# The order of the last loads, finished rows and block halves at the end of a diffusion block with mixture of experts

## The reference

```
x  = x + gx1 * mixer(rmsnorm(x) ...)                 # pooling mixer and gated linear attention
hx = rmsnorm(x, norm2) * (1 + cx2) + sx2
s  = sigmoid(hx @ w_router)                          # 16 experts, top 2 of one group
xb = rows of hx sorted by expert, padded to blocks of 128
yb = (silu(xb @ w1[e]) * (xb @ w3[e])) @ w2[e]       # for each block, e its expert
x  = x + gx2 * (for each token the weighted sum of its two rows of yb)
out = rmsnorm(x, norm_f)
```

## Time and profile before

| | |
|---|---|
| median of 3 runs | 892.17 us (891.77 to 892.59) |
| profiled execution | 892.63 us, its span 890.9 us |
| busy: TensorE, VectorE | 858.4 us (96%), 635.9 us (71%) |
| busy: ScalarE, GpSimd | 415.1 us (47%), 194.5 us (22%) |
| chain that ended last, by engine | PE 78%, DVE 11%, DMA 5% |
| mean granted clock | 0.984 |

### The profile page before, as it was taken

How to read it: one execution, slowest core, us unless ns; L and a number is a source line. 1 busy time by engine, 2 the same in 40 slices (tenths; PEclk the granted TensorE clock), 3 DMA queues, 4 the chain that set the end, 5 groups by cost and what they waited for, 6 DMA issues and landing times.

```text
span 890.9 us, 14102 instructions
## 1 busy us (share of the span) xinstructions
PE 858.4 (96%) x4980; PEld 706.8 (79%) x4981; DVE 635.9 (71%) x907; ACT 415.1 (47%) x597; POOL 194.5 (22%) x225
## 2 busy tenths in 40 slices
PE   8999999999999999999879999999999999999993
PEld 6789878888997567887678888888888888888872
DVE  1678755789777748556875769399936648599995
ACT  3485456201224441232253457378634525487772
POOL 4042001100000101111033323233313222234324
PEclk9999999999999999999969999999999999999997
DMA  9953566511035032222799759979997596699984
GB/s 342 344 179 110 171 194 211 152 43 57 8 142 191 1 142 81 109 79 102 261 338 329 245 170 370 303 245 379 377 361 255 174 307 220 176 342 379 370 331 177
DMA packets 82359, 195.31 MB, mean 219 GB/s; under 512 B 4919, under 2 KB 13324, under 8 KB 82314
## 3 DMA queue, kind: packets, MB, share of 16 engines
q1 hardware_dynamic: 71168, 158.87, 49.6%
q0 software_dynamic: 8272, 25.84, 11.2%
q10 hardware_dynamic: 2874, 10.01, 2.8%
HBM read 169.57 MB, written 25.71 MB: 219 GB/s over the span
## 4 chain that ended last, share of the span: by engine, by line
PE 78%; DVE 11%; DMA 5%; issue 2%; ACT 2%; POOL 1%; ACTq 0%; SPq 0%; POOLq 0%; DVEq 0%
PE ps L2455 16%; PE ps L2443 12%; PE ps L2104 9%; PE ps L2460 8%; PE ps L2107 7%; PE ps L2437 2%; PE ps L2304 2%; DMA raw<-in_w_dram 2%; PE ps L2295 1%; DVE arena L1420 1%; PE ps L2297 1%; PE ps L2296 1%; DMA raw<-x_rows 1%; PE ps L2246 1%; PE ps L2160 1%
## 5 line engine op out<-in xcount | busy, mean ns | idle before, releaser
L1144 ACT ACTIVATE wah<-raw 128x2048 fp32r (+1 forms) x32 | 61.4, 1919 | 65.6 <-issue 32.8
L1853 DVE TENSOR_TENSOR wbl<-raw,wbh 128x2048 fp32r<-128x2048 f32 x32 | 73.1, 2288 | 5.2 <-ACT wbh L1144 4.5
L2443 PE MATMUL ps<-w2h,hTh 128*128 128x512 f32 x184 | 76.1, 413 | 0.5 <-DVE hTl L1863 0.5
L2455 PE MATMUL ps<-wbh,xTh 128*128 128x512 f32 x184 | 73.9, 402 | 0.0
L2455 PE MATMUL ps<-wah,xTh 128*128 128x512 f32 x184 | 72.3, 393 | 0.0
L775 POOL DMA_INDIRECT x_rows<-late_rows,block_dst x21 | 49.9, 2375 | 102.8 <-DVE late_rows L1868 102.8
L2443 PE MATMUL ps<-w2h,hTl 128*128 128x512 f32 x184 | 72.3, 393 | 0.0
L2443 PE MATMUL ps<-w2l,hTh 128*128 128x512 f32 x184 | 72.1, 392 | 0.0
L2455 PE MATMUL ps<-wal,xTh 128*128 128x512 f32 x184 | 72.1, 392 | 0.0
L1853 DVE TENSOR_TENSOR wal<-raw,wah 128x2048 fp32r<-128x2048 f32 x30 | 68.8, 2292 | 4.5 <-issue 3.2
L1853 DVE TENSOR_TENSOR w2l<-raw,w2h 128x2048 fp32r<-128x2048 f32 x32 | 71.8, 2282 | 0.0
(11 more groups left out here) (412 smaller groups left out, 2178.0 us busy)
## 6 DMA issues: line engine op xcount, KB each, us to landing
raw<-in_w_dram SPq DMA_DIRECT2D x64, 1024.0 KB
raw<-in_w_dram SPq DMA_DIRECT2D x16, 2048.0 KB
arena<-in_w_mod_dram SPq DMA_DIRECT2D x32, 512.0 KB, 4.1
arena<-in_x_dram SPq DMA_DIRECT2D x16, 512.0 KB, 9.7
arena<-in_w_mod_dram SPq DMA_DIRECT2D x3, 2048.0 KB, 13.7
arena<-in_w_in_dram SPq DMA_DIRECT2D x6, 1024.0 KB, 6.8
x_rows<-arena ACTq DMA_DIRECT2D x9, 512.0 KB, 3.1
hx_rows<-arena ACTq DMA_DIRECT2D x9, 512.0 KB, 4.4
```

Of the source, the lines that this page charges most:

```text
L1144: act.activation(high_half, raw_half, ACT.Copy).then_inc(w_high[j], 1)
L1853: dve.tensor_tensor(low_half, raw_half, high_half.bitcast(F32), ALU.subtract).then_inc(w_split[j], 1)
L2443: ins = pe.matmul(out_ap, parts[l][:, lhs], w_parts[w][:, cols], start=start and n == 0, stop=stop and n == 2)
L2455: pe.matmul(ps[:, 2 + j, :], xTh[:, k * P:(k + 1) * P], w[:, k * HALF:(k + 1) * HALF], start=(k == 0 and w is wh), stop=False)
```

## The change

SyncE's eight row loads are issued before the norm's row, and the wait for the split of expert 15's weights, which the norm's row needs, moves behind them. ScalarE squares tile 6 before the silu of the last block's second half, squares tile 7 and copies `hidden_high(last, 1)` before it scales tile 3. VectorE forms the first half of the last block and the sum of `early_x` before it waits for the norm's row and finishes tile 0; `hidden_low(last, 0)` then stands before tile 1, tile 2 and `hidden(last, 1)` before the two products of tile 3, and the finish of `early_x` goes behind the last sum. Nothing is added or taken away.

```diff
@@ SyncE
             sp.wait_ge(w_split[2], 2 * (NE - 1))
             sp.wait_ge(w_split[1], 2 * (NE - 1))
-            sp.wait_ge(w_split[1], 2 * NE - 1)
-            sp.dma_start(nfb, norm_f ...).then_inc(S["nf_loaded"], 16)
             sp.wait_ge(S["rows_added"], 1)
             for t in range(NX):
                 sp.dma_start(x2_row[t], x_dram[t * P:(t + 1) * P, :]).then_inc(row_loaded[t], 16)
+            sp.wait_ge(w_split[1], 2 * NE - 1)
+            sp.dma_start(nfb, norm_f ...).then_inc(S["nf_loaded"], 16)
@@ ScalarE
             row_square(5)
+            row_square(6)
             gate_half(last, 1)
-            row_square(6)
+            row_square(7)
+            hidden_high(last, 1)
             act.wait_ge(S["last_sum"], 2)
             act.wait_ge(S["pow_ready"], NT + NX + FIN_ORDER.index(ACT_ROW) + 1)
             act.activation(x2_row[ACT_ROW], ...)
-            hidden_high(last, 1)
-            row_square(7)
             end_square(NX, early_x)
@@ VectorE
-            dve.wait_ge(S["nf_loaded"], 16)
-            finish(0, x2_row[0])
             hidden(last, 0)
-            finish(1, x2_row[1])
-            hidden_low(last, 0)
             dve.wait_ge(S["y_ready"], 2 * last + 2)
             dve.wait_ge(S["gathered"], 16 * last + 48)
             dve.tensor_tensor(early_x, early_x, ysb[:, 0, :], ALU.add).then_inc(S["last_sum"], 1)
+            dve.wait_ge(S["nf_loaded"], 16)
+            finish(0, x2_row[0])
+            hidden_low(last, 0)
+            finish(1, x2_row[1])
+            finish(2, x2_row[2])
+            hidden(last, 1)
...
             dve.tensor_tensor(weighted[:, HALF:], weighted[:, HALF:], nfb[:, HALF:], ALU.mult).then_inc(S["last_sum"], 1)
-            hidden(last, 1)
-            finish(2, x2_row[2])
             hidden_low(last, 1)
             for t in range(ACT_ROW + 1, NX):
                 finish(t, x2_row[t])
-            finish(NX, early_x)
             for h in range(2):
                 dve.wait_ge(S["l2_done" if h else "l2_half"], last + 1)
                 weigh_half(last, h, last_y)
...
                 dve.tensor_tensor(last_x[:, cols], ps[:, h, :], last_y[:, cols], ALU.add).then_inc(S["last_sum"], 1)
 
+            finish(NX, early_x)
             dve.wait_ge(S["last_sum"], 3)
```

More of the change, by code:

```diff
@@ L634, in _ @@
             sp.wait_ge(w_split[1], 2 * (NE - 1))
-            sp.wait_ge(w_split[1], 2 * NE - 1)
-            sp.dma_start(nfb, norm_f.rearrange("(o n) -> o n", o=1).partition_broadcast(P)).then_inc(S["nf_loaded"], 16)
             sp.wait_ge(S["rows_added"], 1)
@@ L639, in _ @@
                 sp.dma_start(x2_row[t], x_dram[t * P:(t + 1) * P, :]).then_inc(row_loaded[t], 16)
+            sp.wait_ge(w_split[1], 2 * NE - 1)
+            sp.dma_start(nfb, norm_f.rearrange("(o n) -> o n", o=1).partition_broadcast(P)).then_inc(S["nf_loaded"], 16)
             for t in range(NX):
```

## The result

The changed kernel takes 893.32 us (median of 21 runs, 891.68 to 896.84), the kernel before 892.01 us (21 runs, 890.32 to 892.59): ratio 1.0021, 95% interval 1.0015 to 1.0028, so slower, by just over the 0.2% that the prediction took as the least that can be told. The medians are 1.3 us apart; the ratio says a little more, because five of the 21 runs lie at 894.8 or above and none of the kernel before does. Predicted were 893.7 us, range 891.0 to 895.9.

What follows compares the result with a forecast made beforehand. TensorE is 78% of the wait chain, but VectorE's last sum, GpSimd's root and the nearly level store path set the end. Loads -1.4, norm's row +11.4 swallowed to +0.4, stores' end +1.5: 893.7 us, range 891.0 to 895.9.

Steps and rivals of the forecast that it cites:

- Loads: SyncE's queue: first row goes out at 849.45, 1.4 us earlier; the norm's row, last of nine, lands at 866.5.
- T: Time of VectorE's first finished row, set by the norm's row landing: 866.5 us instead of 855.
- the upper bound: Latest landing of the norm's row, 867.3, if the slow start belongs to the first load and the broadcast both.
- VectorE: VectorE's chain from T to the last sum takes 13.2 us, so the sum is written at 879.7: +0.4 us.
- the clock rival: TensorE's clock falls to half in the last block, costing 1.2 us of matmuls; 894.4 us in all; chance 0.25.
- The stores: Eighth plain row store lands late and holds GpSimd's first indirect store: +0.8 or +1.9 us, taken as +1.5.
- the short tail: Eighth row store lands 1.2 us behind the end of its data, at 881.7; first indirect store +0.8 us.
- the long tail: Landing 2.3 us behind the data, at 882.8, put down to an instruction fetch on one DMA engine; +1.9 us.
- the fetch moves with the block: The instruction fetch moves by 2 us with the last block, into the full stretch of row stores again.
- my fourth point: Beside the root's path runs the plain stores' path: eighth lands at 880.6, 0.7 us before the root is done.
- `finish(NX)` behind the last sum "costs nothing": VectorE has 2.0 us between sum and root; this row and the product take 1.8; 1.2 us without that cover.
- ScalarE "nothing": ScalarE's new order: first gate_half some 1.5 us earlier, squares 6 and 7 cost nothing; value nothing.

Runs made afterwards that it cites:

- e3: Changed kernel plus eight full-width matmuls with unused result in TensorE's wait ahead of the last block's second layer; 892.71 us, ratio 1.0006 to the kernel before.
- e4: Changed kernel with the finish of early_x back ahead of the weighed halves; 893.97 us, ratio 1.0018 to the kernel before.
- e9: Changed kernel with ScalarE's order of before, SyncE and VectorE as changed; 894.45 us, ratio 1.0026 to the kernel before.
- e10: Changed kernel with norm's row loaded fourth, finish(0) ahead of the early sum, early_x's finish in two halves with second operand from PSUM; 889.15 us.
- e11: Same as e10, but the two halves of early_x's finish read the norm's row from SBUF as second operand; 889.44 us, ratio 0.9974 to the kernel before.
- e5: Changed kernel with the norm's row as fourth of the nine loads, between rows 2 and 3; 890.68 us, ratio 0.9983 to the kernel before.
- e6: e5 with the finish of early_x back ahead of the weighed halves; 890.93 us, ratio 0.9990 to the kernel before.

## Why the prediction came out near, and which steps failed

**Loads: right.** Anchored at the mark, the first row goes out at 849.42 (predicted 849.45), and the norm's row lands at 865.9 (predicted 866.5, bounds 864.8 to 867.3). The set of nine took 16.5 us from first issue to last landing, against 17.1 before, so T was 0.6 us too late. (The parts of the upper bound add up to 867.0, not 867.3; nothing hangs on it.)

**VectorE: right.** From the first finished row to the end of the last sum it took 13.99 us, 0.65 of it the wait for TensorE: 13.34 us against 13.2. With a full clock (e3) the last sum lies 19.27 behind the mark, 0.06 later than before; predicted was +0.4, less the 0.6 us of T and with 0.14 us more of chain about nothing.

**TensorE: the clock rival occurred**, which I gave 0.25. The fall came 0.7 us behind the first wait, lasted 3.4 us (the stretch in the earlier trace rows shows 3.0), and cost 0.65 us where TensorE meets VectorE, half of the 1.2 us that I gave it: the half rate also filled a second wait of TensorE, 0.25 us here and 0.92 in e3. By the Trainium skill (TensorE: Matmul & The Clock Gate, "The HAM clock gate") activity has to hold the throttle off, so a wait can cost more than its length; this trace agrees, with 2.21 us of waiting and 3.4 us at 0.50, and e4's, 2.14 us of waiting and a clock that stayed at 1.00, shows that it doesn't follow each time.

**The stores: the step that failed.** I let the eighth store's long landing set the end (+1.5 us, the largest term of the sum). It was issued at 875.85 and landed in 3.8 us, not 5.5 as in the earlier trace rows, at 879.7: 1.3 us before GpSimd took the root. In the clock of before that is 880.5, where I had 881.7 with the short tail and 882.8 with the long one. The five rows drained at the rate that I took: 6.45 us at 405 GB/s, where I had 6.4 us at 410. What differed was the start of their data, 0.55 us earlier, and the tail behind the full stretch, 0.6 us, where I had 1.2 as the short one and 2.3 as the long one. No packet of an instruction fetch lay in that stretch (q8 has none from 868 to 880), so the long tail that I moved along with the block did not come.

```profile
872.65:879.10 6.45, 5.58 (x18) 2.96 (x16) 5.80 (x8) 0.93 (x4) 2.20 (x3) 1.00 1.01 405
```

The other traces bear on the fetch. From 780 us until the stores have landed, only three of the thirteen executions have a packet on q8: the kernel before at 872.6, e3 at 873.3 and e9 at 873.4. The eighth store landed in 3.2 to 3.9 us in the ten without one, in 5.5 us in the kernel before and in 4.8 us in e3, where the fetch also fell among the row stores; in e9 it fell at a pause between them, and the store took 3.7 us. Behind the full stretch the DMA engines moved single packets for another 1.6 us before and 0.8 us in e3, and in after for no more than 0.2 us. So the long tail as I explained it is borne out by two traces, though no kernel was made to test it. That the fetch moves with the block was wrong: in after none came. Whether that goes by the kernel or by the execution, one trace of each can't tell. In e3, at the eighth store and at GpSimd's waits for the stores:

```profile
q8 instruction: 1, 0.02, 0.7%
...
out_dram<-raw SPq DMA_DIRECT2D x1, 512.0 KB, 4.8
...
L859 POOLq EVENT_SEMAPHORE  x2: 17/30/42, 881.1 to 881.3; - x2
```

e3 is the one kernel here in which this path bound at all. Everywhere else, but for e10, the first indirect store begins 0.94 or 0.95 us behind the start of the root, at which time GpSimd's waits for the stores pass too; in e3 the eighth landed at 881.3, after the root's start at 881.10, and the indirect store began 1.11 us behind that start, so 0.17 us late. The same reading corrects my fourth point: in the kernel before the landing (880.6) stood 0.2 us before the time at which it would have held GpSimd (880.8), not 0.7.

**`finish(NX)` behind the last sum "costs nothing": wrong**, by 0.4 to 0.5 us. I looked at VectorE's free time only. GpSimd is in that interval too, with the two steps to which the end is tied, and they wait for each VectorE instruction with two SBUF inputs. The Trainium skill says so (SBUF — State Buffer, "Who interferes with whom"): a VectorE instruction whose two inputs are both in SBUF contends with a GpSimd instruction that reads SBUF, and one with at most one such input, outside the two-port modes, does not. e10 and e11 agree (0.19 against 0.58 us for the same step). The rule gives the place a price that I didn't weigh. The place still pays: the sum comes 0.93 us earlier for it (e3 against e4, e5 against e6), so 0.4 us are left.

**ScalarE "nothing": right for the whole change, wrong for the part.** The sum wrote VectorE's chain without a wait for ScalarE, and so it ran. But that it did is the doing of ScalarE's new order; with the old one the chain is 1 us longer (e9).

So the total came out within 0.4 us (+1.5 predicted, +1.07 in the traces, +1.3 in the medians) from a term of +1.5 that did not exist, and from the clock (+0.65) and GpSimd (+0.42), which I had in a rival and at zero. The two are not apart: with a full clock (e3) they are +0.06 and +0.67, of the latter 0.17 the stores. That the sum was near is luck, and no evidence for the store step.

## What to carry to other kernels

A shared operand that every later step needs goes early in its queue: at the first or the fourth place the norm's row left the gain of the engines' new orders standing (-1.2 us), and at the ninth it turned it into a loss of 1.3. A change in several engines' orders is priced with each part alone and together: SyncE's part here cost 5.8 or 2.5 us, depending on the others. Before an instruction is put into an engine's free time, look at what the other engines on the path do in it, GpSimd above all, and set what it costs them against what the move gains.

## What the runs showed of the hardware

- A GpSimd step on one column took 0.19 to 0.27 us where nothing held it and 0.57 to 1.13 us beside VectorE instructions with two SBUF inputs, and ended within 0.05 us of their ends in the rows of after and of e11. Beside a row with one input in PSUM it took 0.19 and 0.26 us (e10).
- A wait of TensorE of 2.21 us amid full-width matmuls was followed by 3.4 us at 1.2 GHz in one execution (e9: 2.36 us and 3.4 us), and one of 2.14 us by none in another (e4). With eight matmuls in the gap the clock stayed at 2.4 GHz in the one trace taken (e3).
- The last of eight row stores (512 KB) landed in 3.2 to 3.9 us in the ten executions without an instruction fetch in that stretch, and in 5.5 us (before) and 4.8 us (e3) where a fetch fell among the stores; in e9 one fell at a pause and it took 3.7 us. This was observed and not tested by a kernel.
